# Expert weights of a fused RWKV/SGU/conv block with grouped mixture of experts: the gate-and-up part reloaded in two transfers of 2 MB in place of four of 1 MB

## The reference, cut to what matters

```python
def expert_block(args):
    xblk, e = args
    h = jax.nn.silu(xblk @ w_gate[e]) * (xblk @ w_up[e])     # 1024 -> 512, twice
    return h @ w_down[e]                                     # 512 -> 1024

yb = lax.map(expert_block, (xb, block_expert)).reshape(rows, d)
y = jnp.zeros((t, d), yb.dtype).at[buf_tok].add(yb * buf_gate[:, None].astype(yb.dtype), mode='drop')
...
x = layer_norm(ALPHA * x + moe_out, ln2_g[l], ln2_b[l])
```

## Time and profile before

| | |
|---|---|
| median of 3 runs | 1092.33 us (1092.11 to 1097.02) |
| the profiled execution: time, span | 1096.18 us, 1094.3 us |
| PE busy | 1000.2 us, 91% |
| DVE, ACT, POOL busy | 43%, 27%, 22% |
| bytes moved by DMA | 256.62 MB, of which q1 240.57 MB |
| mean granted TensorE clock | 0.987 |

### The profile page before, as it was taken

One profiled execution on the slowest core, in us unless ns is written; L12 is line 12 of the kernel. 1 busy time (PEld: TensorE's weight loads), 2 busy tenths in 40 slices (PEclk: granted clock), 3 DMA queues, 4 the chain that ended last, 5 costly groups with the idle time before them and its releaser, 6 DMA issues.

```text
span 1094.3 us, 16700 instructions
## 1 busy us (share of the span) xinstructions
PE 1000.2 (91%) x6130; PEld 461.0 (42%) x6131; DVE 466.7 (43%) x1037; ACT 290.3 (27%) x480; POOL 236.2 (22%) x336
## 2 busy tenths in 40 slices
PE   7999999999999999999999788888888888887774
PEld 3644466456457447544444333333333333332221
DVE  0696452463363464232226534434434443432333
ACT  1113322222232132200014123333333333332321
POOL 3000010010010001023105133333334334333332
PEclk9999999999999999999999999999999999999998
DMA  9422211220221120473836899999999999999992
GB/s 279 122 78 60 75 40 40 58 58 22 58 58 42 39 75 4 155 261 129 342 122 250 296 415 415 408 402 416 415 415 414 416 414 415 415 414 416 416 404 106
DMA packets 96897, 256.62 MB, mean 235 GB/s; under 512 B 17485, under 2 KB 62541, under 8 KB 72017
## 3 DMA queue, kind: packets, MB, share of 16 engines
q1 hardware_dynamic: 85024, 240.57, 57.7%
q0 software_dynamic: 11024, 13.20, 3.5%
q10 hardware_dynamic: 800, 2.15, 0.5%
HBM read 260.66 MB, written 21.23 MB: 258 GB/s over the span
## 4 chain that ended last, share of the span: by engine, by line
PE 52%; SPq 16%; DMA 14%; DVE 9%; issue 6%; POOL 1%; ACT 1%; POOLq 0%; DVEq 0%; PEld 0%; ACTq 0%; PEldq 0%
SPq L478 15%; PE proj L1429 12%; PE proj L1388 11%; PE proj L1608 5%; PE bank L1519 5%; PE bank L1597 5%; DMA out<-raw 3%; DMA y_rows<-const,raw 3%; DMA arena<-w_gu 3%; DMA xT_sb<-w_gu 3%; PE bank L1732 2%; DMA pass_sb<-x_rows,raw 2%; PE proj L1396 2%; PE proj L1407 1%; DVE arena L982 1%
## 5 line engine op out<-in xcount | busy, mean ns | idle before, releaser
L1429 PE MATMUL proj<-xT_sb,ring 128*128 128x512 f32 x384 | 182.1, 607 | 0.0
L1732 PE MATMUL bank<-arena 128*64 128x512 f32 x544 | 122.2, 596 | 17.4 <-PE bank L1753 9.8
L1314 DVE TENSOR_TENSOR raw<-bank,const 128x512 f32<-128x512 f32 x33 | 22.9, 693 | 242.6 <-DMA out<-raw 240.7
L1388 PE MATMUL proj<-xT_sb,ring 128*128 128x512 f32 (+1 forms) x272 | 119.1, 594 | 0.0
L1429 PEld LDWEIGHTS proj<-xT_sb,ring 128*128 128x128 f32 x384 | 68.3, 189 | 68.3 <-issue 64.8
L1732 PEld LDWEIGHTS bank<-arena 128*64 128x64 f32 x544 | 42.9, 137 | 96.6 <-issue 82.9
L1388 PEld LDWEIGHTS proj<-xT_sb,ring 128*128 128x128 f32 (+1 forms) x272 | 50.8, 188 | 64.6 <-issue 64.5
L825 ACT ACTIVATE pass_sb<-bank 128x256 f32<-128x256 f32 x33 | 12.6, 383 | 195.2 <-PE bank L1732 195.2
L516 POOL MEMSET arena<- 64x64 f32 x8 | 1.2, 145 | 291.7 <-DVE arena L999 257.9
L1732 PE MATMUL bank<-gates,arena 128*64 128x512 f32 x256 | 57.4, 597 | 6.8 <-PE bank L1753 4.0
L1519 PEld LDWEIGHTS bank<-arena 64*64 64x64 f32 x1536 | 52.8, 134 | 18.2 <-ACT arena L725 9.1
(11 more groups left out here) (305 smaller groups left out, 1372.7 us busy)
## 6 DMA issues: line engine op xcount, KB each, us to landing
arena<-w_gu SPq DMA_DIRECT2D x64, 1024.0 KB, 22.4
gates<-w_gu SPq DMA_DIRECT2D x32, 1024.0 KB
arena<-w_down SPq DMA_DIRECT2D x24, 1024.0 KB
ring<-w_in SPq DMA_DIRECT2D x42, 512.0 KB, 3.9
gates<-w_down SPq DMA_DIRECT2D x16, 1024.0 KB
branches<-w_down SPq DMA_DIRECT2D x16, 1024.0 KB
xT_sb<-w_gu SPq DMA_DIRECT2D x16, 1024.0 KB
ring<-w_gu SPq DMA_DIRECT2D x16, 1024.0 KB
```

The source lines that it names most:

```text
L1388: ins = pe.matmul(proj[0:w, b, :], ring[:, slot, k, 0:w], xT_sb[:, k, :], start=(k == 0), stop=(k == KT - 1))
L1429: ins = pe.matmul(proj[:, gate_at["bank"], :], ring[:, gate_at["slot"], k, :], xT_sb[:, k, :], start=(k == 0), stop=(k == KT - 1))
L1732: ins = pe.matmul(bank[SLOTS * h:SLOTS * h + SLOTS, 0, :], xeT[:, k % 4, SLOTS * (k // 4):SLOTS * (k // 4) + SLOTS], gu[k // 2][:, k % 2, ...
```

## The change

In `reload`, the four gate-and-up chunks are issued as two DMAs of 2 MB, 16 KB in each partition, since chunks 0 and 1 lie side by side both in memory and in their home, and so do 2 and 3. SP waits for the pair: the DMA for chunks 0 and 1 is issued when the old chunk 1 has been read, where the DMA for chunk 0 needed the old chunk 0 alone. Only the semaphores of chunks 0 and 2 are raised by the pairs. PE waits on these at steps 0 and 4 for the load's number; at steps 2 and 6 it waits on those of chunks 1 and 3 for 16, which the first loads (four single chunks, unchanged) have already given. The down chunks are issued and awaited one by one as before.

```diff
@@ -273,6 +273,8 @@
+        w_pair = [[h[:, at + n * 2 * CHUNK:at + (n + 1) * 2 * CHUNK] for n in range(2)]
+                  for h, at in ((homes[0], 0), (homes[1], 0), (homes[2], 0))] + [[homes[4][:, 0:2 * CHUNK], homes[5][:, 0:2 * CHUNK]]]
@@ -471,10 +473,14 @@
             def reload(e, b, used):
 
-                for c in range(NCH):
+                for c in (0, 2):
+                    sp.wait_ge(s_used, used + c + 3)
+                    src = w_gu[bass.ds(e, 1), :, c * CHUNK:(c + 2) * CHUNK]
+                    sp.dma_start(w_pair[b][c // 2], src.rearrange("a p n -> (a p) n")).then_inc(s_w[b][c], 16)
+                for c in (4, 5):
                     sp.wait_ge(s_used, used + c + 2)
-                    n = c * CHUNK
-                    src = w_gu[bass.ds(e, 1), :, n:n + CHUNK] if n < GU else w_down[bass.ds(e, 1), :, n - GU:n - GU + CHUNK]
+                    n = c * CHUNK - GU
+                    src = w_down[bass.ds(e, 1), :, n:n + CHUNK]
                     sp.dma_start(w_chunk[b][c], src.rearrange("a p n -> (a p) n")).then_inc(s_w[b][c], 16)
@@ -1726,8 +1732,10 @@
                 for k in range(KT):
-                    if k % 2 == 0:
+                    if k % 4 == 0:
                         pe.wait_ge(s_w[b][k // 2], loads)
+                    elif k % 2 == 0:
+                        pe.wait_ge(s_w[b][k // 2], 16)
```

## The result

The changed kernel takes 1135.94 us (median of 4 runs, 1133.36 to 1137.52); the kernel before took 1092.98 in the runs beside them. The ratio is 1.038, with a 95% interval of 1.036 to 1.041: slower by 43 us. That is the top of the forecast's own range (1104 to 1136 us) and 16 us over its point of 1120. The profiled span went from 1094.3 to 1133.9 us, by 39.6.

The account below looks back on a forecast made before the run. PE's 13.5 us passes were taken as bound by loops holding an indirect DMA's latency, and after 985 us by weight loads; 31 X - 12.6 with X = 1.3 gave +27.7, 1120.0 us, range 1104 to 1136 (8 in 10: 1089 to 1147).

Parts of the forecast that it names:

- the mechanism: On the DMA engines, indirect DMAs wait longer behind q1's 16 KB rows, lengthening each pass by 1.3 us.
- the loop: Chain through POOL from one scatter to the next: 13.75 us a pass, half of it an indirect DMA's latency.
- the term X: Latency added to each indirect DMA beside q1's 16 KB rows, lengthening every pass: 1.3 us taken, 0.8 to 1.8 the forecast's range.
- (a) to (c): SP's later issue of pairs, +1.8 us; fewer, longer rows in the stream, -3.3; PE's pair wait in the last pass, +1.8.
- (d): SP issues two DMAs fewer per expert but has time to spare either way: 0.
- (e): Indirect DMAs on other queues wait behind q1's rows, longer with longer rows: 0 to +2.05 us each, 1.3 taken.
- 12 rows: The 3.8 us an indirect DMA loses under full q1, read as about 12 rows of 8 KB at 0.31 us.
- the four turns: Only four of an indirect DMA's turns on an engine get longer, two thirds behind 16 KB rows: +0.8 us a DMA.
- the full-wait rival: All 12 q1 rows ahead of an indirect DMA count: +2.05 us a DMA, +51 us, 1143 us; chance 0.28.
- the lower end: The lower positive bound for an indirect DMA's added wait, with only four turns longer: +0.8 us.
- R2: The indirect DMAs' wait does not depend on q1's row length: +0.3 us, 1092.6 us, no change; chance 0.23.
- R3: No added wait for indirect DMAs, and the stream of loads gains more: -5.8 us, 1086.5 us, faster; chance 0.13.

Follow-up runs that it names:

- The run with pairs alone: SyncE and PE wait for pairs as in the changed kernel, but each pair is two 1 MB DMAs of 8 KB rows; 1097.41 us, 1.002 against the kernel before.
- the 2 MB run: Sets 0 to 2 reload gate and up in two 2 MB DMAs of 8 KB rows, chunks 0 and 2, 1 and 3; 1099.86 us, 1.005 against the kernel before.
- the run with late long rows: The kernel before with 16 KB rows and pairs only for experts 24 to 31, single chunks for the others; 1107.31 us, ratio 1.014.
- the filler run: The changed kernel with eight small extra matmuls on PE ahead of each turn of the next tokens; 1140.37 us, 1.041 against the kernel before.

## Why the prediction was right, and where its sizes were off

The sign, the mechanism and the loop were right; the time came out at the top of the forecast's range because the term X was too small, and it stayed inside because smaller errors ran the other way.

(a) to (c): a delay of SP, of PE in the last pass, and a gain by fewer rows. They were said to vanish if the passes grow, and they did: there is no wait for `w_gu`. The run with pairs alone, where passes don't grow, has 2 us for the waits where the text had 1.8 + 1.8. The queue did run empty near 700 us: SP issues nothing from 689.7 to 709.21 us, and the scatter of 707.22 us lands in 2.38 us; it cost nothing, as weights were ahead of PE. The stream's gain can hardly be seen in its rate: 415 GB/s between 720 and 980 us before, 415 again in the 2 MB run, 417 after. The forecast that the DMA share would fall late was right only for the last two slices. The chain was to be full of `y_rows<-const` and `out<-raw`; between 700 and 1000 us it has the tokens' gather for 22%, that scatter for 20% and `out<-raw` for 6%.

(d) SP's issue: nothing to pay, as said.

(e), the term X, carried the prediction, and it is the one that was mis-sized: 1.3 was taken, the mean of four DMAs is 1.97, and the scatter that closes the loop has 2.21. The reading of the loop held: 13.44 and 15.65 us against 13.58 and 15.83 measured. Errors of size met that pull both ways. In passes 8 to 26 each pass lost 2.4 us (43.4 us in 18 passes) where the text had 1.3: +20 us over the forecast. In passes 1 to 8, where q1 isn't yet full, it lost 0.46 and not 1.3: -6. The last six took 88.8 us as forecast (6 x 14.8), but by luck: they are 13.4, 15.3, 18.9, 14.4, 13.4 and 13.4 us, two long ones and three at PE's own pace, and not six of 14.8. The last pass's own waits, which the sum had forgotten, gave 2.4. Together 27.7 + 20 - 6 - 2 is the 39.6 us of the spans.

Why was X larger? The prediction took 12 rows' time as the wait, and bounded X by the four turns and by all twelve rows. The packets of the trace allow the split. For the gather of `y_rows`, which has no other indirect DMA right in front of it, medians in us after its issue:

| rows on q1 | first packet | last semaphore packet | landed |
|---|---|---|---|
| none | 1.64 | 2.37 | 2.71 |
| 4 KB | 4.26 | 5.92 | 6.39 |
| 8 KB (before) | 4.22 | 6.10 | 6.45 |
| 16 KB (after) | 4.22 | 7.45 | 7.87 |
| 32 KB | 4.44 | 10.79 | 11.19 |

The wait until the first packet grows by 2.6 us as soon as q1 is full, and then doesn't depend on the row: 8 of the "12 rows" were not rows. What the full-wait rival rested on is refuted. Why the first packet waits is open; what is refuted is that this part grows with the row. The time between the first and the last packet goes 0.73, 1.66, 1.88, 3.23, 6.35 us. Less the 0.73 of an empty q1, and divided by what a row takes (0.164, 0.313, 0.614, 1.219 us in the packets), that is 5.7, 3.7, 4.1 and 4.6 rows; the first is too high because a part of q1's rows in that run are the 8 KB ones of the down chunks. So about one row of q1 goes between each of the DMA's five packets on an engine, as the lower end had it. With 32 KB rows it can be seen: in most of these gathers the packets come in groups 1.2 us apart, the time of one row. (The prediction read these packets as four rows and a semaphore; by their bytes, at most 4096, each of the four carries up to two rows of 2 KB. That changes none of its counts.)

Two things may have made it more than that end's 0.8 us. I had counted two thirds of the turns as long, but nearly all are: 14 of 16 scatters between 730 and 985 us take over 7.5 us. That pass and stream keep step, so that each pass meets the same stretch, would explain it; it was only argued. And three of the four are issued 2 us apart, so that the later ones may queue behind the earlier ones' longer turns: they have +1.9 to +2.4 where the isolated one has +1.4. No run separates the two.

The Trainium skill, page DMA: Bandwidth & Descriptors, section "Queues, rings and completion order", has an engine drain a packet of 9 to 17 descriptors before it switches. The direction was right: longer rows, longer turns. That the turns are whole packets agrees with the trace, in which each packet of q1 is one row. That a packet holds 9 to 17 descriptors is not borne out. Nine rows of 16 KB would be 5.5 us a turn; the whole DMA lost 1.4 to 2.4. Here an engine changes queues after about one row. The page's gain for larger transfers, which the prediction set aside, was absent in all runs: 2 MB of 8 KB rows ran at the same 415 GB/s as 1 MB.

The full-wait rival named 1143 us and the measurement lies nearer to it than to 1120, but its mechanism is the refuted one. R2 needed X under 0.4, R3 a faster stream; neither came.

What stays open: why the first packet waits 2.6 us longer under a full q1 of any row length; why the indirect DMAs of the run with late long rows take up to 11.7 us where after stays under 9.9; and how much of the loss is the clock's own. After has the lower clock for 58 us between 620 and 1080, before for 10. The rounds from scatter to scatter leave 7 of 42 us for everything but the latency, and the filler run, which kept the clock up, is 4 us faster than after in passes 8 to 26. So the clock has some microseconds of the 43, and the latency most of them.

## What to carry to other kernels

Where a loop of the kernel holds a small DMA's latency, look at the row length of whatever streams beside it: each of the small DMA's packets waits for about one row of the stream, so fewer and longer rows for the stream are paid for by the loop. Read the loop from the chain (latency plus the rest) and set it against the engine's own rhythm; when they are level, a longer latency counts nearly in full. And don't take the cost of a few long rows as their share of the whole: the DMAs that they hit waited longer here than under long rows throughout.

## What the runs showed that I had not expected

- 4 KB rows save nothing in latency (6.4 us against 6.5 and 6.6) and cost the stream 2% (407 against 415 GB/s).
- An indirect DMA under a full q1 has its first packet 4.2 us after issue, with 4, 8 and 16 KB rows alike (4.4 with 32 KB), and 1.6 with q1 empty.
- One reload in four with long rows costs 11 us, a quarter of the whole loss, although in its trace the scatter's median is nearly unchanged (6.7 against 6.6): the loss is in the eight passes that are hit.
- Memsets of 0.41 us ahead of an indirect DMA lengthened its loop by 0.2 us only: they largely took the place of 0.54 us that stood ahead of the DMA instruction anyway.
